# Two norm borders of a fused two-block kernel: ScalarE writes odd tiles' high halves, one weight split behind two tiles, fillers ahead of the second block

## What is computed

```python
x = first_block(...)                                  # its last product is "out1"
h = _rms_norm(x, mix_norm_pre[l]) * (1.0 + sc1[:, None]) + sh1[:, None]
y = _token_mixer(h, ...)                              # its first product is "q_a"
x = x + g1[:, None] * _rms_norm(y, mix_norm_post[l])
h = _rms_norm(x, ffn_norm_pre[l]) * (1.0 + sc2[:, None]) + sh2[:, None]
y = _conv_ffn(h, ...)                                 # its first product is "up0"
```

## Time and profile before

| | |
|---|---|
| median of 3 runs | 2544.72 us |
| the profiled execution | 2542.83 us |
| its span, first to last instruction | 2541.0 us |
| TensorE busy | 2514.4 us, 99% of the span |
| VectorE busy | 1927.6 us, 76% |
| ScalarE busy | 1292.0 us, 51% |
| mean granted clock of TensorE | 0.998 |

### The profile page before, as it was taken

The page is one execution under the profiler, slowest core; times in us unless marked ns, Lnnn a source line. Parts: engine busy times, 40 slices in busy tenths (PEclk is TensorE's granted clock), DMA queues, the critical chain, the costliest instruction groups (busy, mean ns, idle before and its releaser), DMA issues.

```text
span 2541.0 us, 35172 instructions
## 1 busy us (share of the span) xinstructions
PE 2514.4 (99%) x13860; PEld 2155.5 (85%) x13860; DVE 1927.6 (76%) x2745; ACT 1292.0 (51%) x1752; POOL 8.4 (0%) x84
## 2 busy tenths in 40 slices
PE   8999999999999999999999999999999999999998
PEld 7888888888888888888788888888888888888886
DVE  7788676887767678676667877886888887788855
ACT  7644556554455655454445455544644443444443
POOL 0000000000000000000000000000000000000000
PEclk9999999999999999999999999999999999999999
DMA  8688555778755576865566888888566678966664
GB/s 282 206 294 276 152 165 156 242 257 291 247 154 167 152 233 214 257 193 174 166 216 199 293 270 270 271 267 277 144 195 189 187 229 304 277 198 200 200 190 140
DMA packets 528118, 558.73 MB, mean 220 GB/s; under 512 B 17729, under 2 KB 455106, under 8 KB 527826
## 3 DMA queue, kind: packets, MB, share of 16 engines
q1 hardware_dynamic: 527954, 556.48, 70.2%
HBM read 552.22 MB, written 2.10 MB: 218 GB/s over the span
## 4 chain that ended last, share of the span: by engine, by line
PE 98%; DVE 1%; DMA 0%; ACT 0%; issue 0%; DVEq 0%; SPq 0%; ACTq 0%
PE ACC L522 49%; PE ACC L527 24%; PE ACC L468 7%; PE ACC L469 7%; PE ACC L470 7%; PE SC L1350 1%; PE OU L1401 1%; PE SC L1368 1%; PE SC L1409 1%; PE ACC L495 0%; PE OU L1860 0%; PE OU L1390 0%; PE SC L1341 0%; PE OU L1536 0%; DVE X L970 0%; DMA RAW<-in_w_mem_kv 0%
## 5 line engine op out<-in xcount | busy, mean ns | idle before, releaser
L522 PE MATMUL ACC<-XH,WH 128*128 128x512 f32 x5296 | 1687.3, 400 | 11.2 <-DVE XH L1236 11.2
L594 ACT ACTIVATE WH<-RAW 128x1024 fp32r<-128x1024 f32 (+1 forms) x852 | 897.0, 1057 | 1068.2 <-PE ACC L527 694.8
L603 DVE TENSOR_TENSOR WL<-RAW,WH 128x1024 fp32r<-128x1024 f32 (+1 forms) x852 | 1032.7, 1220 | 497.7 <-ACT WH L594 496.2
L527 PEld LDWEIGHTS ACC<-XH,WL 128*128 128x128 f32 x5296 | 996.5, 188 | 235.7
L527 PE MATMUL ACC<-XH,WL 128*128 128x256 f32 x5296 | 1042.8, 278 | 0.0
L522 PEld LDWEIGHTS ACC<-XH,WH 128*128 128x128 f32 x5296 | 812.4, 189 | 28.9 <-issue 14.0
L2080 DVE SCALAR_TENSOR_TENSOR RAWMOD<-RAWMOD,CSILU 128x1024 f32<-128x1024 f32 x192 | 233.9, 1218 | 1.0 <-DMA RAWMOD<-in_w_mod_t 0.9
L468 PE MATMUL ACC<-WH,XH 128*128 128x512 f32 x384 | 151.0, 393 | 0.0
L469 PE MATMUL ACC<-WL,XH 128*128 128x512 f32 x384 | 149.6, 389 | 0.0
L470 PE MATMUL ACC<-WH,XH 128*128 128x512 f32 x384 | 149.5, 389 | 0.0
L468 PE MATMUL ACC<-WH,AH 128*128 128x512 f32 x352 | 137.3, 390 | 0.0
(11 more groups left out here) (278 smaller groups left out, 1378.5 us busy)
## 6 DMA issues: line engine op xcount, KB each, us to landing
RAW<-in_w_in SPq DMA_DIRECT2D x408, 512.0 KB, 4.5
RAWMOD<-in_w_mod_t SPq DMA_DIRECT2D x192, 512.0 KB, 5.1
RAW<-in_w_up SPq DMA_DIRECT2D x176, 512.0 KB, 4.7
RAW<-in_w_out SPq DMA_DIRECT2D x96, 512.0 KB, 5.2
RAW<-in_w_down SPq DMA_DIRECT2D x88, 512.0 KB, 4.9
RAW<-in_w_mem_kv SPq DMA_DIRECT2D x32, 512.0 KB, 5.4
RAW<-in_w_branch_gla SPq DMA_DIRECT2D x32, 512.0 KB, 5.0
RAW<-in_w_branch_attn SPq DMA_DIRECT2D x16, 512.0 KB, 4.9
```

Of the source, the lines that this page charges most:

```text
L522: return pe.matmul(bank, k.WH[:, w % RING, kc, cols], x, start=tile == 0, stop=False)
L527: return pe.matmul(bank[:, 0:T], k.WL[:, w % RING, kc, cols], x[:, 0:T], start=False, stop=tile == tiles - 1)
L594: act.activation(k.WH[:, slot, :, 0:width], k.RAW[:, r % RAWS, :, 0:width], ACT.Copy).then_inc(k.hi_ready, 1)
L603: dve.tensor_tensor(k.WL[:, slot, :, 0:width], k.RAW[:, k.plan.unit_load[unit] % RAWS, :, 0:width], k.WH[:, slot, :, 0:width].bitcast(F32) ...
```

## The change

At both borders the high halves of the odd tiles are written by ScalarE straight from PSUM, with the same gain and shift as the tile itself, just before it writes the tile to PR. ScalarE does so only after `hi_input` has counted all tiles before, so after VectorE's high half of the even tile. VectorE writes the high halves of even tiles, and still all low halves. VectorE's low half of the third weight unit moves from ahead of tile 0 to ahead of tile 2. In `up0` TensorE no longer waits for it before tile 0, but inside tile 0 ahead of the second bank. Ahead of the turns for `q_a`, 16 fillers run.

```diff
 def pe_first_tiles(pe, k, stage):
     for phase in range(2):
-        pe.wait_ge(k.split_ready, stage.unit0 + phase + 3)
+        pe.wait_ge(k.split_ready, stage.unit0 + (1 if phase == 0 else 4))
...
             for s in range(2):
                 w = phase + 2 * s
+                if tile == 0 and s == 1:
+                    pe.wait_ge(k.split_ready, stage.unit0 + 3)
...
+def stage_inputs(k, stage):
+
+    return k.plan.f_in if stage.name == "mix_out" else k.plan.h2
...
 def act_token_norm(act, k, stage, chain):
...
         act.wait_ge(k.turned_normed, KT * n + f + 1)
+        if f % 2 == 1:
+            act.wait_ge(k.hi_input, stage_inputs(k, stage) + f)
+            act.activation(k.XH[:, f, 0:T], turned_tile(k, f), ACT.Identity,
+                           scale=gains[:, f:f + 1],
+                           bias=shift[:, f:f + 1]).then_inc(k.hi_input, 1)
         act.activation(k.PR[:, 16 + f, :], turned_tile(k, f), ACT.Identity,
                        scale=gains[:, f:f + 1], bias=shift[:, f:f + 1]).then_inc(k.scaled, 1)
...
 def pe_keep_warm(pe, k, stage):
     pe.wait_ge(k.evacuated, stage.pair0 - 1)
-    pe.wait_ge(k.tok_squared, 14)
-    for n in range(WARM):
+    pe.wait_ge(k.tok_squared, 14 if stage.name == "up0" else 6)
+    for n in range(WARM if stage.name == "up0" else WARM // 2):
...
 def dve_token_norm(dve, k, stage, chain):
...
     units = stage.pairs * stage.per_pair
-    token_split_ahead(dve, k, stage, units - 2, dve_split)
     for f in range(KT):
-        if f == 6:
-            token_split_ahead(dve, k, stage, units - 1, dve_split)
+        if f in (2, 6):
+            token_split_ahead(dve, k, stage, units - (2 if f == 2 else 1), dve_split)
         hi, normed = k.XH[:, f, 0:T], k.PR[:, 16 + f, :]
         dve.wait_ge(k.scaled, scaled + f + 1)
-        dve.tensor_scalar(hi, normed, 1.0, None, ALU.mult).then_inc(k.hi_input, 1)
+        if f % 2 == 0:
+            dve.tensor_scalar(hi, normed, 1.0, None, ALU.mult).then_inc(k.hi_input, 1)
         dve.wait_ge(k.hi_input, first + f + 1)
         dve.tensor_tensor(k.XH[:, f, T:2 * T], normed, hi.bitcast(F32),
                           ALU.subtract).then_inc(k.xh_ready, 1)
...
         pe_stage(pe, k, s[f"out{l}"])
+    pe_keep_warm(pe, k, s["q_a"])
     for f in range(4):
         pe_turn_normed(pe, k, 0, f)
```

More of the change, by code:

```diff
@@ L985, in dve_token_norm @@
                                  accum_out=k.TOKS[:, 13:14]).then_inc(k.row_squared, 1)
-        rstd, row, scaled, first = k.row_rstd, 18, KT, k.plan.f_in
+        rstd, row, scaled = k.row_rstd, 18, KT
     else:
-        rstd, row, scaled, first = k.tok_rstd, 16, 0, k.plan.h2
+        rstd, row, scaled = k.tok_rstd, 16, 0
+    first = stage_inputs(k, stage)
     for b, half in ((0, 0), (1, 0), (1, 1)):
```

## The result

The changed kernel takes 2553.01 us, the median of 7 runs (2552.39 to 2553.53). The kernel before took 2544.88 us beside it (2542.88 to 2547.39, 7 runs). The ratio is 1.0034, with a 95% interval from 1.0024 to 1.0043: 8.1 us slower, against 7.55 forecast. The profiled execution has 2553.33 us and a span of 2551.6 us, 10.6 us above the one before.

What follows compares the result with a forecast made beforehand. TensorE bounds the kernel before; changed, the ScalarE-VectorE chain bounds both borders. Second border +4.30 and first +3.25 make 7.55 us on 2542.83, so 2550.4; with 1.89 us to the median, 2552.3 us; range 2547.5 to 2556.0.

Steps and rivals of the forecast that it cites:

- rival 4: Behind the borders, a later stage takes the delay up, so the change doesn't reach the end: about 2545; chance 0.03.
- the queues: Loads on SP held up by later weight splits at the borders: put at 0, at most 1 us a border.
- The price of the write: ScalarE's added high-half activations, eight at each border: 0.567 us each, 0.455 us in a row.
- Rival 2: ScalarE's added write at the borders takes 0.363 instead of 0.567 us: +4.2 us, 2548.9; chance 0.12.
- The round trip: At both borders ScalarE and VectorE wait for each other in each pair of tiles: 1.84 us per pair.
- the list of 17.70 us: ScalarE's work from its first tile to the fifth unit's high half, at each border: 14.70 + 0.95 + 2.05 us.
- Splits on the chain: VectorE's two weight splits, ahead of tiles 2 and 6, each delay the chain 1.03 us, 2.05 for both.
- 2.35 us behind the list: The fifth unit's high half on ScalarE (1.06 us) and low half on VectorE (1.22 us), each with a handoff.
- The fillers: 16 fillers at the first border keep full clock, delay transposes 0.77 us; without the other parts, 1.6 us gain.
- The moved split: At the second border, tile 0's second bank waits for it: a new gap of about 1.8 us inside tile 0.
- Rival 1: TensorE stays the bound: first border gains 1.6 us, second loses some 0.5; -1.1 us, 2543.6; chance 0.07.
- Rival 3: The clock falls at the second border, 3.4 us on top of the chain: +10.9 us, 2555.7; chance 0.12.

Runs made afterwards that it cites:

- kernel 1: The kernel before with only the 16 fillers ahead of `q_a` added: 2543.89 us, ratio 0.9998 to the kernel before.
- kernel 5: The changed kernel without the fillers ahead of `q_a`: 2551.18 us, ratio 1.0032 to the kernel before.
- kernel 3: The kernel before with only the moved weight split: 2543.88 us, ratio 0.9998 to the kernel before.
- Kernel 4: The changed kernel with ScalarE's high halves counted on a semaphore of their own: 2546.00 us, ratio 1.0005 to the kernel before.
- kernel 6: The kernel before with, at the first border only, 12 fillers, ScalarE's fourth-unit half ahead of tile 6 and VectorE's splits moved: 2542.78 us, ratio 0.9996 to before.
- kernel 2: The kernel before with only ScalarE's high halves of odd tiles added: 2550.33 us, ratio 1.0029 to the kernel before.
- kernel 7: Kernel 6 with 36 instead of 32 fillers ahead of `up0`: 2542.64 us, ratio 0.9995 to the kernel before.
- Kernel 8: Kernel 7 with one filler between each two of the eight decays' matmuls in `kv_a`: 2550.16 us, ratio 1.0028 to the kernel before.

## Why the prediction was right, and where it was off

- **TensorE's path between two points decides.** Right: behind the second border both kernels take 730.9 us, and the two borders carry 8.5 us, against 8.1 us of the medians. That also rules out rival 4, a later stage that takes the delay up, and bears out the 0 us that the queues were given.
- **The price of the write.** Taken from line 725, 0.567 us; measured 0.56, and 0.45 to 0.47 from start to start. Rival 2, the cheap write of 0.363 us, is out.
- **The round trip.** 1.84 us a pair was forecast, 1.90 measured. The term that was too small is the handoff: I used 0.035 us for both directions, from VectorE to VectorE. From ScalarE to VectorE it was 994.02 - 993.98 = 0.04, from VectorE to ScalarE 994.41 - 994.31 = 0.10. Over eight pairs that is 0.5 us a border: the list of 17.70 us took 18.18 at the first border and 18.17 at the second.
- **Splits on the chain.** 1.03 us each was forecast, 1.02 measured. 2.35 us behind the list was forecast, 1014.06 - 1011.60 = 2.46 measured, and 2.46 at the second border too.
- **The fillers.** Alone 1.6 us of gain forecast, 1.8 measured (kernel 1), and none of it under the round trip (kernel 5). The half clock is gone from the first border, as forecast. I had them end too late: the transposes were to start 993.80 - 989.75 = 4.05 us after the last matmul of `out1`, and started 993.00 - 989.21 = 3.79 us after it, so ScalarE's first tile came 0.24 us sooner than forecast (4.21 us after that matmul, not 4.45).
- **The sum.** 7.55 us, with 0.95 more for the handoffs, 0.22 more behind the lists and 0.24 less for the fillers, is 8.5 us, which is what the borders measured. The last error hid a part of the others at the first border; the second, where it has no part, missed by 0.6 us.
- **The moved split.** A new wait inside tile 0 of 1.8 us forecast, 1.6 measured; alone 0.9 us (kernel 3).
- **Rival 1**, TensorE stays the bound, doesn't describe the change. Kernel 4, without the wait on `hi_input`, comes near it at the first border (1.3 us gained, 1.6 by the rival), but not in the median.
- **Rival 3**, the clock at the second border: it did fall (0.81 and 0.62 below), but its 3.4 us on top did not come. The changed kernel with 3.4 us of half clock takes 29.93 us and kernel 5 with 6.8 us takes 29.92.

The stretches of the changed kernel at the second border:

```profile
1802.00:1805.00 3.00, 1.37 (x6) 1.23 (x6) 2.21 (x5) 1.56 (x5) 0.00 (x0) 0.81 0.03 7
1805.00:1808.00 3.00, 3.00 (x13) 2.62 (x13) 1.31 (x4) 2.58 (x5) 0.00 (x0) 0.62 0.58 173
```

By the Trainium skill, "TensorE: Matmul & The Clock Gate", section "HAM oscillation — how this bites in real kernels", idle gaps between bursts of matmuls can throttle the clock; this trace agrees in so far as the clock fell behind gaps of 1.3 and 1.6 us. The gaps that the section tells of are longer than these, though; the same gaps that brought a fall in kernels 1 and 6 brought none in the kernel before, and the last section has a fall without any gap. Whether a fall costs anything is another question, and rows answer it: nothing that can be seen where TensorE waits for ScalarE and VectorE, 1.3 to 1.6 us where TensorE is the bound (26.3 and 26.6 us in kernels 1 and 6, against 25.05 before, with the same instructions at that border).

The medians differ by 8.1 us, the borders of the two profiles by 8.5 and their spans by 10.6. The profiled execution of the kernel before had no fall of the clock outside the first border; if some of its other runs had one, as those of kernels 1 and 6 with the same code at the second border did, its median holds a part of that time. The mean granted clock of each run bears this out (last section): those near its median of 2544.88 us have 0.997, the profiled one 0.998. Where the clock fell in them was not shown.

## What to carry to other kernels

A count shared by two engines that must rise in order is a wait, also where the data need none; here 6.8 of 8.1 us hung on it (kernel 4). Before an engine is given a share of another's work, write down the loop of waits that it closes and put everything that interrupts either engine on that loop; a semaphore for each engine keeps the work and drops the loop. Gains measured alone don't add: the fillers' 1.8 us vanish as soon as TensorE is no longer the bound.

## What the runs showed that I had not expected

The granted clock falls at a third place, in `kv_a`, where TensorE is not idle (kernel 5: busy for all 86 us from 1014 to 1100). It multiplies the decays there, eight matmuls that use 16 of the array's 128 rows. The profiled execution of the kernel before stayed at full clock, as did kernel 2; the changed kernel and kernels 3 to 5 had half clock there for 3.4 us, kernels 1, 6 and 7 for 6.8 us. The same stretch in the kernel before and in kernel 1 (clock after the five busy times):

```profile
1056.00:1059.00 3.00, 3.00 (x15) 2.59 (x14) 1.23 (x1) 0.90 (x1) 0.00 (x0) 1.00 1.02 208
```

```profile
1056.00:1059.00 3.00, 3.00 (x10) 2.02 (x9) 0.00 (x0) 0.00 (x0) 0.00 (x0) 0.51 1.08 208
```

TensorE is busy for all 3.00 us in both. With 3.4 us of it the way between the borders took 775.3 to 776.7 us, with 6.8 us 777.0 to 777.6, against 774.0 and 774.1 without. So in these executions, of kernels with the same code there, the way between the borders differed by up to 3.6 us, most of it from this, and up to 1.6 us more came at the second border. The spread of the kernel before, 2541.9 to 2548.6 in 30 runs, is of that size, and it goes with the clock: the 11 runs with a mean granted clock of 0.998 took 2541.90 to 2543.15 us, the 9 with 0.997 took 2543.70 to 2544.88, the 10 with 0.996 or 0.995 took 2545.37 to 2548.55. Where the clock fell in them is not known, since only one execution was profiled.

This is also where the changed kernel's 2.6 us between the borders lie. Kernels 3 and 5, with the same 3.4 us and no wait of TensorE in the attention, have 1.2 and 1.3 of them; kernel 4 waits 0.4 us there and has 1.9; the changed kernel waits 0.9 and has 2.6. So 1.3 us go with the fall and the rest about with the waits. Whether these waits come of the change is not shown: kernel 1, whose high halves are all VectorE's, has one of 0.4 us as well.

What makes the clock fall there stays open. Kernel 8 was to settle it and did not: 128-row fillers in between did not hold the clock, so the 16 rows alone are not shown to be the cause.
